# In the second block, the scan and the attention of the older head come ahead of the preparation and the pair norms of the newer one in each round

## The reference

```python
hn = rms_norm_2(x, w_norm)
proj = hn @ w_in                                   # q_a k_a v_a z_a b_a a_a | q_b k_b v_b z_b
q_a, k_a, v_a = silu(causal_conv4(q_a, k_a, v_a))
q_a = l2_norm(q_a) * 128 ** -0.5; k_a = l2_norm(k_a)
o_a = gated_delta_rule_chunked(q_a, k_a, v_a, g, beta)   # 4 heads of 128
o_a = rms_norm_2(o_a, gdn_norm_w) * silu(z_a)
q_b, k_b = rope(rms_norm_2(q_b)), rope(rms_norm_2(k_b))  # 4 heads of 2 x 64
o_b = softmax(q_b0 k_b0) v_b - lam * softmax(q_b1 k_b1) v_b   # causal
o_b = rms_norm_2(o_b, subln_w) * (1 - lam_init) * silu(z_b)
x = x + concat(o_a, o_b) @ w_out
```

## Time and profile before

| | |
|---|---|
| median of 3 runs | 1284.21 us (1282.32 to 1287.08) |
| profiled execution | 1276.16 us, of which the span of the profile is 1274.7 us |
| TensorE | busy 1174.2 us, 92% of the span |
| VectorE | busy 646.0 us, 51% |
| ScalarE | busy 446.1 us, 35% |
| GpSimd | busy 153.5 us, 12% |
| mean granted TensorE clock | 0.970 of 2.4 GHz |

### The profile page before, as it was taken

How to read it: one execution, slowest core, us unless ns; L and a number is a source line. 1 busy time by engine, 2 the same in 40 slices (tenths; PEclk the granted TensorE clock), 3 DMA queues, 4 the chain that set the end, 5 groups by cost and what they waited for, 6 DMA issues and landing times.

```text
span 1274.7 us, 14227 instructions
## 1 busy us (share of the span) xinstructions
PE 1174.2 (92%) x5664; PEld 922.6 (72%) x5664; DVE 646.0 (51%) x1041; ACT 446.1 (35%) x744; POOL 153.5 (12%) x123
## 2 busy tenths in 40 slices
PE   6999999999978999999999987888879878978998
PEld 2787878788745888888888863677668667757776
DVE  3444444446335777777732215533653564465374
ACT  5232323234433344444432213421242352343341
POOL 1000000000240000000000013032122203303310
PEclk9999999999989999999999998897989989999999
DMA  7112222212311223333233331111110111111111
GB/s 299 59 60 83 66 67 67 67 66 83 99 50 46 89 97 99 100 100 99 93 112 109 106 123 34 49 34 33 34 50 34 33 50 34 33 50 34 34 33 67
DMA packets 25313, 91.63 MB, mean 72 GB/s; under 512 B 2848, under 2 KB 3104, under 8 KB 25120
## 3 DMA queue, kind: packets, MB, share of 16 engines
q1 hardware_dynamic: 22608, 82.32, 19.8%
q0 software_dynamic: 1200, 6.10, 1.3%
q10 hardware_dynamic: 1440, 2.31, 0.5%
HBM read 88.63 MB, written 2.10 MB: 71 GB/s over the span
## 4 chain that ended last, share of the span: by engine, by line
PE 78%; DVE 11%; ACT 6%; issue 3%; POOL 1%; DMA 0%; ACTq 0%; DVEq 0%
PE PS L467 19%; PE PS L470 18%; PE PS L468 18%; PE PS L687 3%; PE PS L558 2%; PE PS L745 2%; ACT Wh L1516 1%; PE PS L580 1%; PE PS L742 1%; PE PS L896 1%; DVE C L1410 1%; PE PS L898 1%; PE PS L897 1%; PE PS L676 1%; DVE Wl L925 1%
## 5 line engine op out<-in xcount | busy, mean ns | idle before, releaser
L467 PE MATMUL PS<-Hh,Wh 128*128 128x512 f32 x928 | 389.0, 419 | 32.8 <-DVE Hl L939 27.2
L470 PE MATMUL PS<-Hh,Wl 128*128 128x512 f32 x928 | 367.6, 396 | 0.0
L468 PE MATMUL PS<-Hl,Wh 128*128 128x512 f32 x928 | 367.1, 396 | 0.0
L925 DVE TENSOR_TENSOR Wl<-raw,Wh 128x1024 fp32r<-128x1024 f32 x156 | 189.9, 1222 | 177.6 <-ACT Wh L1516 175.4
L467 PEld LDWEIGHTS PS<-Hh,Wh 128*128 128x128 f32 x928 | 177.5, 191 | 105.0 <-issue 41.9
L470 PEld LDWEIGHTS PS<-Hh,Wl 128*128 128x128 f32 x928 | 177.0, 191 | 39.2
L468 PEld LDWEIGHTS PS<-Hl,Wh 128*128 128x128 f32 x928 | 177.8, 192 | 29.9 <-issue 0.7
L1516 ACT ACTIVATE Wh<-raw 128x1024 fp32r<-128x1024 f32 x156 | 162.2, 1048 | 51.3 <-PE PS L470 47.0
L467 PE MATMUL PS<-Ah,Wh 128*128 128x512 f32 x176 | 69.8, 396 | 0.0
L468 PE MATMUL PS<-Al,Wh 128*128 128x512 f32 x176 | 69.8, 396 | 0.0
L470 PE MATMUL PS<-Ah,Wl 128*128 128x512 f32 x176 | 69.8, 396 | 0.0
(11 more groups left out here) (285 smaller groups left out, 1637.1 us busy)
## 6 DMA issues: line engine op xcount, KB each, us to landing
raw<-in_w_units SPq DMA_DIRECT2D x156, 512.0 KB, 3.4
relb<-in_rel POOLq DMA_DIRECT2D x1, 2048.0 KB, 8.5
out<-X ACTq DMA_DIRECT2D x8, 256.0 KB, 2.0
X<-in_x POOLq DMA_DIRECT2D x3, 512.0 KB, 9.7
mats<-in_mats POOLq DMA_DIRECT2D x1, 832.0 KB, 4.7
window<-in_window POOLq DMA_DIRECT2D x1, 544.0 KB, 12.1
X<-in_x SPq DMA_DIRECT2D x1, 512.0 KB, 4.3
rope<-in_rope POOLq DMA_DIRECT2D x1, 512.0 KB, 5.2
```

Source lines behind the costliest of these rows:

```text
L467: pe.matmul(bank, Wh[:, s, w], rhs[0](r), start=first and j == 0, stop=False)
L468: pe.matmul(bank, Wh[:, s, w], rhs[1](r), start=False, stop=False)
L470: ins = pe.matmul(bank, Wl[:, s, w], rhs[0](r), start=False, stop=last and end)
L925: dv.tensor_tensor(Wl[:, s, :], raw[:, s, :], Wh[:, s, :].bitcast(F32), sub).then_inc(unit_split, 1)
```

## The change

In each of the four engines' programs that have chains, the list of a stage is put together in the other order: scan and diff of head b first, then pair_norms and prep of head a. For stage 0 (no head b) and for the last part (no head a) nothing changes. No instruction is added or removed.

```diff
@@ TensorE, VectorE, ScalarE and GpSimd alike @@
         def chains_of(st, a, b):
             own = [pair_norms(st, a), prep(st, a)]
-            return own + ([scan(st, b), diff(st, b)] if b is not None else [])
+            return ([scan(st, b), diff(st, b)] if b is not None else []) + own
```

## The result

The changed kernel took 1275.84 us (median of 6 runs, 1271.85 to 1277.18), the kernel before 1282.86 us (6 runs on the same chip, 1281.36 to 1287.08): ratio 0.9938, 95% interval 0.9914 to 0.9962. In medians the gain is 7.0 us, three times the sum of 2.3 us.

A forecast was written before the change was run, and what follows sets the result against it. TensorE, busy for 92% of the span, was taken to bound the kernel. Gains of 0.6 + 1.4 + 0.3 = 2.3 us off the median 1284.21 gave 1281.9 us, own range 1281.2 to 1282.6, wider range 1278 to 1286.5.

The forecast's parts named there:

- the sum of 2.3 us: Whole forecast gain: 0.6 us from St's clears, 1.4 from stage 1's late round, 0.3 from stages 2 and 3.
- the base: The time the gain was taken from: median 1284.21 us, though the terms were read from a profiled execution of 1276.16.
- St's clear: Start of a stage: clear ahead of the gs copies cuts TensorE's wait by 0.20 us, 0.6 us over three stages.
- Second round: Rope product L1357 ahead of three VectorE preparation operations fits into the 2.39 us idle ahead of L1222; costs nothing.
- Late round, stage 1: Oa and output ahead of the sums bring dense work back sooner: 1.4 us gained, between 0.8 and 2.0.
- Stages 2 and 3: Late round there: the new order removes the 0.19 us wait at the sums, 0.15 us each, 0.3 in both.
- Whether the gain lasts: Other engines work from TensorE's products, so later waits move up with them; gain kept in full.
- rqk behind Wd: Late round on VectorE: the norm's rqk moves behind Wd, 0.8 us or more of cover left; costs nothing.
- (a): Clock shifts for the better in stages 1 to 3: 4.4 us gained, 1279.8 us; chance 0.22.
- (b): Clock falls behind the sums in stages 2 and 3 too: +0.7 us, 1284.9 us; chance 0.14.
- (c): Wait at the sums only moves, stage 1's slow stretch swallows most: 1.1 us gained, 1283.1 us; chance 0.16.
- (d): rqk is late, so the turn of V waits 0.3 us in each stage: 1282.8 us; chance 0.06.

The follow-up runs named there:

- e1: The kernel before once more, no edit: median 1283.7 us, ratio 0.9993 to before.
- e2: The kernel before with the new order only in rounds up to 5 (clear of St, rope product L1357): median 1278.68 us, ratio 0.9957 to before.
- e4: The changed kernel again, no edit: median 1276.19 us, ratio 0.9933 to before.
- e10: The changed kernel a third time, no edit: median 1276.26 us, ratio 0.9972 to before.
- e11: The changed kernel a fourth time, no edit: median 1276.56 us, ratio 0.9965 to before.
- e3: The kernel before with the new order only in rounds after 5 (Oa and output ahead of the sums): median 1275.55 us, ratio 0.9940 to before.
- e9: The kernel before with the late rounds' new order in TensorE's program only: median 1279.86 us, ratio 0.9985 to before.
- e12: The kernel before a third time, no edit: median 1283.36 us, ratio 0.9997 to before.
- e7: The changed kernel plus three unused 512-column products ahead of TensorE's wait for the third Wd, all four heads: median 1292.28 us, ratio 1.0133 to before.
- e8: As e7, plus two more such products ahead of the wait for Od's turn in stages 1 to 3: median 1286.83 us, ratio 1.0099 to before.

## Why the prediction was wrong

**The step that failed is the base.** The sum was made on one profiled execution, and the prediction said of it that it "lies 8 us under the median of 1284.21, which is the number to forecast, so 1284.21 - 2.3". That carries the gain from an execution at clock 0.970, with 23.8 us at 0.50 in the stages, over to executions at 0.965 or less with 44 to 51 us. So the forecast itself put the clock's share at nothing. The 8 us were noted, but not asked what they were. They are clock: between before's own two profiles (spans of 1274.7 and 1286.5 us, clocks 0.970 and 0.962) the clock makes 10.6 of the 11.8 us. In e1 it is lost in slow stretches at other places, one of them across the very round that the change edits: the late round of stage 2, costed at 0.15 us, is away from dense work for 5.21 us in e1 and 2.85 in the changed kernel. Of the 6.1 us between 1281.9 and 1275.84, 4.7 are the gain (7.0 for 2.3) and 1.4 the base, since 1284.21 was the median of three runs and before had 1282.86 beside the changed kernel.

**The size, in means over all runs.** Before is at 1281.5 us and the changed kernel at 1276.6, a gain of 4.8 us (ratio 0.996). Of that the clock (0.9685 against 0.9670) is 1.9 us by the line, and 2.9 us are left at equal clock, near the 2.3 of the sum. Set only against before's runs beside them, e4, e10 and e11 give 8.7, 3.9 and 4.4 us, 5.0 on average over their 30 runs, again with 2.9 at equal clock. In medians the gain is 6.7 us, since before's median sits in its slower heap, and the first comparison, 8.0 us in means, drew none of before's better runs. The clocks of those six are not on record; by the line, an estimate, 3.5 of the 8.0 us are the order and 4.5 the clock. So the recorded 0.9938 is on the large side; e10 and e11 came out at 0.9972 and 0.9965. Split by a line, the two parts are not sharp: at clock 0.968 the changed kernel is 5.3 us ahead, at 0.969 3.0, at 0.972 2.3, and its three runs at 0.964 (1287.1 us) are behind before's (1284.4).

**St's clear:** right. The wait is 0.14 us shorter each (0.20 forecast), and e2 shows the early part alone. It came out at 1.0 us at equal clock, 0.6 forecast, within the error. (e2's further 3.9 us are clock.)

**Second round:** right. L1357 costs nothing, the wait ahead of L1222 is 1.34 us, and no wait stands ahead of the readers. The timeline of the changed kernel:

```profile
893.62 0.69 DVE L1222 TENSOR_TENSOR head_DT<-PS,gcum 128x512 f32<-128x512 f32 x1 [1.34 <-PE PS L676]
...
898.85 1.29 POOL L2027 TENSOR_TENSOR head_Kr<-head_Kr,tmp 128x512 f32<-128x512 f32 x1
...
902.39 1.13 PE L841 MATMUL PS<-head_Kr,head_Qb 64*128 64x512 f32 x4
```

**Late round, stage 1:** right in mechanism. Dense work is away 3.04 us (3.2 forecast), and of the 1.4 us of gain 1.1 are there net, since the dense products ahead end later. The wait of 0.46 us at the sums didn't come, because the dense products ahead run at the lower clock to their end and the squares are ready; the low stretch stands where stages 2 and 3 had it. **Stages 2 and 3:** 2.85 and 2.77 us (1148.81 to 1151.58), against 2.89 and 3.03 in before's own profile (in stage 3 from 1147.64, where the wait begins, to 1150.67):

```profile
1147.83 2.14 PE L708 MATMUL PS<-ones,sq 128*128 128x1 f32 x16 [0.19 <-ACT sq L1727]
```

That is 0.04 and 0.26 us, together the 0.3 that was forecast, as long as before has its good course. **Whether the gain lasts:** in this pair of profiles not in full. Stage 2 is 0.4 us longer than before's, with the slow stretch behind the wait for Od's turn that before's first profile lacks there.

**rqk behind Wd:** right. It starts at 940.14, V's turn (L682 on C) at 941.91 without a wait. On before's time (1.79 us less, by the clears of St) these are 938.35 and 940.12, where 938.8 and 939.6 to 940.4 were forecast.

**The rivals.** (a) has the right kind and nearly the size: its 4.4 us are near the 4.8 and 5.0 us of all the runs, and too small for the 7.0 of the first comparison. Its places are half wrong. Stage 1's second stretch went, but stages 2 and 3 didn't get stage 1's short stretch; stage 1 got their long one. What before loses in its slower executions, the double stretch across the sums and the ones at L773, stands in no rival. (b), the clock falling behind the sums in each stage, did not come with Oa first; it is near to what before itself does in e1. (c) and (d) fell: e3 alone gives 2.7 us at equal clock where (c) had some 0.5 for the late round, and there is no wait for V. The rule from the Trainium skill that the prediction weighed (TensorE: Matmul & The Clock Gate, section "What's actually happening": a free-running monitor) fits what was seen: the same kernel has several courses of the clock. No run shows what picks one.

**What stays open.** Whether the order gives the clock's part of the gain, or the executions drew it. The changed kernel is at 0.968 in most runs, and no run shows why. The six profiles with Oa's work between the dense products and the sums have no double stretch, but all six are of executions at 0.968 or more; e9 has that order and five of its twelve runs are at 0.965, three runs of the changed kernel are at 0.964, and no trace of such a run was taken. e2 has a mean clock 0.003 above before's without that order, and e12's spread was no wider than the changed kernel's. And in e4 and e10 the same kernel won 4.3 and 0.6 thousandths of clock over before, so the clock's 1.9 us is an average that a single comparison may miss.

## What to carry to other kernels

When the profiled execution and the median differ by more than the change is expected to give, first find out what the difference is: profile the old kernel again until an execution near the median is in hand, and read the edited place there. Compare mean clocks of the timed runs as well as times, and divide the gain into what is left at equal clock and what the clock gave. Fill a wait on the bounding engine with work that must be done anyway; a slow stretch that lies under another engine's chain costs little (0.55 us in e7's stage 2), and pushing it out may put it where it costs half its length.

## What the runs showed of the hardware

- One kernel, nothing changed, one core at a time on three chips, took 1270.4 to 1291.4 us over 118 runs, and the mean granted clock (0.976 to 0.960) accounts for all but a scatter of 1.3 us.
- The granted clock fell not only behind waits. In e1, stages 1 and 3, and in e7, stage 2, it fell to 0.50 within 16 passes of two columns (L773), with TensorE busy at full clock ahead of them: in e1, stage 1, for 3.93 of the 4 us from 976 to 980, and the fall came between 980 and 981. In the changed kernel the same instructions met 1.00 throughout, so such a group alone doesn't decide it.
- The 16 passes of one column (L708) take 1.84 us at clock 1.00 and 3.57 us at 0.50: these small products pay for the lower clock in full.
- Removing time at the lower clock is not the same as saving time when it takes added products: e8 had a third less of it in its profile than the changed kernel (20.4 against 30.6 us in the stages), for 14.1 us of added products there, and its median was 9.5 us above that of before on the same chip.
